# Four PSUM banks for the projection units, three staging slots and a gate row summed in sixteen pieces

## Time and profile before

| what | value |
|---|---|
| median of 3 runs | 865.06 us |
| profiled execution, its own time | 870.05 us |
| its span, first to last instruction | 868.2 us |
| PE busy | 772.1 us, 89% |
| DVE, ACT, POOL busy | 517.9, 455.3, 393.0 us |
| mean granted TensorE clock | 0.956 |

### The profile page before, as it was taken

How to read it: one execution, slowest core, us unless ns; L and a number is a source line. 1 busy time by engine, 2 the same in 40 slices (tenths; PEclk the granted TensorE clock), 3 DMA queues, 4 the chain that set the end, 5 groups by cost and what they waited for, 6 DMA issues and landing times.

```text
span 868.2 us, 9916 instructions
## 1 busy us (share of the span) xinstructions
PE 772.1 (89%) x3468; PEld 614.3 (71%) x3468; DVE 517.9 (60%) x716; ACT 455.3 (52%) x749; POOL 393.0 (45%) x405
## 2 busy tenths in 40 slices
PE   6596898999779889889998899699989699999996
PEld 2275687888668768777776787477668478888885
DVE  4389752646873878595776333665534477666633
ACT  4265642887755875766774675334525253434311
POOL 0268553475555763765546446424300235252521
PEclk9897899999988999999998999899999999999999
DMA  9994013245524254343443123344328765858541
GB/s 367 352 298 136 25 38 122 61 105 134 157 70 119 72 165 152 107 129 102 147 143 103 55 92 112 110 134 134 107 80 322 243 222 183 286 170 264 172 134 74
DMA packets 89073, 130.09 MB, mean 150 GB/s; under 512 B 22752, under 2 KB 54112, under 8 KB 87488
## 3 DMA queue, kind: packets, MB, share of 16 engines
q1 hardware_dynamic: 84656, 115.44, 40.7%
q0 software_dynamic: 4368, 14.03, 5.8%
HBM read 91.17 MB, written 38.27 MB: 149 GB/s over the span
## 4 chain that ended last, share of the span: by engine, by line
PE 44%; ACT 15%; DVE 14%; issue 10%; POOL 7%; DMA 6%; SPq 4%; ACTq 0%; POOLq 0%; DVEq 0%
PE bank L1443 14%; PE bank L1444 14%; PE bank L1445 14%; SPq L403 2%; ACT L942 2%; ACT Qb L943 2%; DVE Qb L1267 2%; ACT bank L944 2%; ACT Ib L930 2%; DMA wraw<-in_w_in 2%; DVE gacc L1120 1%; DVE xg L1153 1%; DVE xc L1120 1%; DVE xTl L1171 1%; DVE Ib L1257 1%
## 5 line engine op out<-in xcount | busy, mean ns | idle before, releaser
L1443 PE MATMUL bank<-xTh,wh 128*128 128x512 f32 (+1 forms) x592 | 239.3, 404 | 40.8 <-ACT ustage L917 11.6
L1445 PE MATMUL bank<-xTh,wl 128*128 128x512 f32 (+1 forms) x592 | 236.1, 399 | 0.0
L1444 PE MATMUL bank<-xTl,wh 128*128 128x512 f32 x576 | 231.9, 403 | 0.0
L1443 PEld LDWEIGHTS bank<-xTh,wh 128*128 128x128 f32 x592 | 116.1, 196 | 68.9 <-issue 42.2
L1445 PEld LDWEIGHTS bank<-xTh,wl 128*128 128x128 f32 x592 | 115.5, 195 | 24.7
L1444 PEld LDWEIGHTS bank<-xTl,wh 128*128 128x128 f32 x576 | 112.9, 196 | 23.8 <-issue 0.2
L1443 PE MATMUL bank<-xTh 128*128 128x512 f32 (+1 forms) x272 | 106.8, 392 | 14.1 <-DVE xTl L1391 7.2
L1445 PE MATMUL bank<-xTh,xTl 128*128 128x512 f32 x256 | 99.9, 390 | 0.0
L1444 PE MATMUL bank<-xTl,xTh 128*128 128x512 f32 x256 | 99.7, 390 | 0.0
L917 ACT ACTIVATE ustage<-bank 128x512 f32<-128x512 f32 x56 | 33.5, 600 | 120.1 <-PE bank L1445 116.0
L569 POOL TENSOR_SCALAR xTh<-yb 128x512 fp32r<-128x512 f32 x32 | 19.8, 619 | 122.1 <-DVE yb L1389 122.1
(11 more groups left out here) (189 smaller groups left out, 1520.1 us busy)
## 6 DMA issues: line engine op xcount, KB each, us to landing
scratch_u<-ustage SPq DMA_DIRECT2D x72, 256.0 KB, 2.9
wraw<-in_w_in SPq DMA_DIRECT2D x18, 512.0 KB, 4.2
wm<-in_w_mod SPq DMA_DIRECT2D x8, 1024.0 KB, 11.7
xg<-in_x SPq DMA_DIRECT2D x16, 512.0 KB, 8.8
yb<-scratch_y SPq DMA_DIRECT2D x32, 256.0 KB, 3.1
gb<-scratch_u SPq DMA_DIRECT2D x32, 256.0 KB, 4.4
xres<-in_x SPq DMA_DIRECT2D x16, 512.0 KB, 4.8
out<-tout SPq DMA_DIRECT2D x16, 512.0 KB, 2.9
```

What stands on the lines that cost most here:

```text
L1443: mm(out, wh_, xh_, start=first, stop=False)
L1444: mm(out, wh_, xl_, start=False, stop=False)
L1445: return mm(out, wl_, xh_, start=False, stop=last)
```

## The change

- The units of the middle (units 8 to 67, `WIDE`) go in turn through four banks, 0, 1, 6, 7, so that a unit waits for the evacuation of the one four before it. The others keep two banks.
- `gr` is one pair, banks 2 and 3. `one_minus_a2` writes its result over `Qb` in SBUF, the root is taken there, and the product with `Ib` reads it there. `gates(q)` waits for `one_minus_a2(q-1)` instead of `scans(q-2)`.
- `ustage` has three slots, with a semaphore each.
- The gate row's weights come in sixteen pieces of 128 x 4 x 128, each summed in its own step, 3 to 18. The rule for where a piece is loaded is as before, and so is the wait for the sum of the piece before it; a `dve.wait_ge` is added behind each sum.
- In the tail the LayerNorm root is taken in place in `lvar` and read from there (`lsd` is gone); the next variance waits for the products that read it; the first mean waits for `one_minus_a2(19)`; the first two pooling products wait for the evacuation of the wide units.

```diff
+U_SLOTS = 3
...
-GATE_STEP = [3 + 2 * m for m in range(8)]
+WIDE = range(N_CU + 2 * NCH, N_CU + GATES_AFTER[-1] + 1)
+PU_BANK = [(0, 1, 6, 7)[U % 4] if U in WIDE else U % 2 for U in range(N_CU + len(UNITS))]
+
+
+def evacuations_before(U):
+
+    earlier = [V for V in range(U) if PU_BANK[V] == PU_BANK[U]]
+    return earlier[-1] + 1 if earlier else 0
+
+
+GATE_STEP = [3 + m for m in range(16)]
 GATE_PIECE_AT = [GATES_AFTER[q - 1] + 1 for q in GATE_STEP]
...
-        wgp = a3.take("wgp", [P, KD, P])
+        wgp = a3.take("wgp", [P, KD // 2, P])
...
-        pu = bank[0:2]
-        gr = [bank[2:4], bank[6:8]]
+        pu = [bank[b] for b in PU_BANK]
+        gr = bank[2:4]
...
                 for o in range(2, NT_IN):
                     if n == LAST_OF[o - 2]:
                         load_w(o + 2)
-                for m in range(KD):
+                for m in range(2 * KD):
                     if n == GATE_PIECE_AT[m]:
                         if m:
                             sp.wait_ge(s_ga, m)
-                        sp.dma_start(wgp[:], w_mod[8 + m // 2, :, :, m % 2 * P:m % 2 * P + P]).then_inc(s_wg, 16)
+                        b, h = divmod(m, 2)
+                        part = w_mod[8 + b // 2, :, h * KD // 2:(h + 1) * KD // 2, b % 2 * P:b % 2 * P + P]
+                        sp.dma_start(wgp[:], part).then_inc(s_wg, 16)
...
-                if U >= 2:
-                    act.wait_ge(s_us[U % 2], 16 * (U // 2))
+                if U >= U_SLOTS:
+                    act.wait_ge(s_us[U % U_SLOTS], 16 * (U // U_SLOTS))
...
-                    r = gr[q % 2][d][:, 0:n]
-                    a.activation(r, r, ACT.Sqrt).then_inc(s_rt, 1)
+                    root = Qb[:, d, 0:n]
+                    a.activation(root, root, ACT.Sqrt).then_inc(s_rt, 1)
...
-                    r = gr[q % 2][d][:, 0:n]
-                    stt(r, Qb[:, d, 0:n], 1.0, r, ALU.add, ALU.mult).then_inc(s_m2, 1)
+                    stt(Qb[:, d, 0:n], Qb[:, d, 0:n], 1.0, gr[d][:, 0:n], ALU.add, ALU.mult).then_inc(s_m2, 1)
...
-                    link(v.tensor_tensor(out=I, in0=I, in1=gr[q % 2][d][:, 0:n], op=ALU.mult))
+                    link(v.tensor_tensor(out=I, in0=I, in1=Qb[:, d, 0:n], op=ALU.mult))
...
-                acc = gacc[:, m * P:(m + 1) * P]
-                link(v.tensor_scalar(acc, wgp[:, 0, :], cs[:, 0:1], None, ALU.mult))
-                for k in range(1, KD - 1):
-                    link(stt(acc, wgp[:, k, :], cs[:, 2 * k:2 * k + 1], acc, ALU.mult, ALU.add))
-                k = KD - 1
-                stt(acc, wgp[:, k, :], cs[:, 2 * k:2 * k + 1], acc, ALU.mult, ALU.add).then_inc(s_ga, 1)
+                b, h = divmod(m, 2)
+                acc = gacc[:, b * P:(b + 1) * P]
+                for k in range(KD // 2):
+                    scale = cs[:, 2 * (h * KD // 2 + k):2 * (h * KD // 2 + k) + 1]
+                    if h == 0 and k == 0:
+                        ins = v.tensor_scalar(acc, wgp[:, k, :], scale, None, ALU.mult)
+                    else:
+                        ins = stt(acc, wgp[:, k, :], scale, acc, ALU.mult, ALU.add)
+                    if k < KD // 2 - 1:
+                        link(ins)
+                ins.then_inc(s_ga, 1)
+                dve.wait_ge(s_ga, m + 1)
...
-                if U >= 2:
-                    pe.wait_ge(s_ev, U - 1)
+                if evacuations_before(U):
+                    pe.wait_ge(s_ev, evacuations_before(U))
...
                 if q:
                     pe.wait_ge(s_sig, 4 * q)
-                if q >= 2:
-                    pe.wait_ge(s_st, 2 * (q - 1))
+                    pe.wait_ge(s_m2, 2 * q)
```

More of the change, by code:

```diff
@@ L128, in mixer_kernel @@
         wl = fixed.take("wl", [P, 2, KD, P], f32r)
-        ustage = fixed.take("ustage", [P, 2, CH])
+        ustage = fixed.take("ustage", [P, U_SLOTS, CH])
         prm = fixed.take("prm", [P, N_PAR])
@@ L269, in mixer_kernel @@
         s_pu, s_ev = sem("unit_done"), sem("unit_evacuated")
-        s_us = [sem(f"u_stored{b}") for b in range(2)]
+        s_us = [sem(f"u_stored{b}") for b in range(U_SLOTS)]
         s_gz, s_gw, s_gwh, s_gwl = sem("gatew_zeroed"), sem("gatew_in"), sem("gatew_hi"), sem("gatew_lo")
@@ L444, in store_u @@
                 if U < N_CU:
[L445 removed]
+                    dst, src = uc_dram[U], ustage[:, U % U_SLOTS, 0:CTX]
                 elif o == "conv":
[L447 removed]
+                    dst, src = cv_dram[c], ustage[:, U % U_SLOTS, 0:NPH]
                 elif ORDER[o] in CONV_TILES:
                     dst = phases(u_dram[ORDER[o]], NPH)[:, :, c * CH // PHASES:(c + 1) * CH // PHASES]
[L450 removed]
+                    src = phases(ustage[:, U % U_SLOTS, :], CH // PHASES)
                 else:
[L452 to L453 removed]
+                    dst, src = u_dram[ORDER[o], :, c * CH:(c + 1) * CH], ustage[:, U % U_SLOTS, :]
+                sp.dma_start(dst, src).then_inc(s_us[U % U_SLOTS], 16)
             def load_conv_w(j):
@@ L627, in load_v @@
                     U = unit_of(V_LRU + t, NCH - 1)
-                    for back in (0, 1):
-                        pool.wait_ge(s_us[(U - back) % 2], 16 * ((U - back) // 2 + 1))
+                    for back in range(U_SLOTS):
+                        pool.wait_ge(s_us[(U - back) % U_SLOTS], 16 * ((U - back) // U_SLOTS + 1))
                     off = a - (c * CH - 2)
@@ L715, in load_ln @@
                 else:
-                    for U in range(N_CU + CONV_AT[-1] - 1, N_CU + CONV_AT[-1] + 1):
-                        pool.wait_ge(s_us[U % 2], 16 * (U // 2 + 1))
+                    for U in range(N_CU + CONV_AT[-1] + 1 - U_SLOTS, N_CU + CONV_AT[-1] + 1):
+                        pool.wait_ge(s_us[U % U_SLOTS], 16 * (U // U_SLOTS + 1))
                 part = slice(n * CH // PHASES, (n + 1) * CH // PHASES)
@@ L1045, in ln_root @@
                     act.wait_ge(s_lzn, 2 * m)
-                a.activation(lsd[:], lvar[:], ACT.Sqrt, bias=lnepsc).then_inc(s_lsd, 1)
+                a.activation(lvar[:], lvar[:], ACT.Sqrt, bias=lnepsc).then_inc(s_lsd, 1)
             def ln_swish(m):
@@ L1368, in ln_norm @@
                 dve.wait_ge(s_lsd, n + 1)
-                link(v.reciprocal(lsd[:], lsd[:]))
+                link(v.reciprocal(lvar[:], lvar[:]))
                 for i in range(2):
                     z = lr[:, n % 2, i, :]
-                    v.tensor_tensor(out=z, in0=z, in1=lsd[:], op=ALU.mult).then_inc(s_lzn, 1)
+                    v.tensor_tensor(out=z, in0=z, in1=lvar[:], op=ALU.mult).then_inc(s_lzn, 1)
             def ln_lo(n):
@@ L1507, in gates @@
                     pe.wait_ge(s_sig, 4 * q)
-                if q >= 2:
-                    pe.wait_ge(s_st, 2 * (q - 1))
+                    pe.wait_ge(s_m2, 2 * q)
                 for m in range(4):
                     d = 0 if s == 0 else m // 2
-                    b = gi_[m // 2] if m % 2 else gr[q % 2][m // 2]
+                    b = gi_[m // 2] if m % 2 else gr[m // 2]
                     ins = mm3(b[:, 0:n], gwh[:, m, :], gwl[:, m, :], sph[:, d, 0:n], spl[:, d, 0:n], True, True)
@@ L1577, in _ @@
                         pe.wait_ge(s_pye, n - 1)
+                    else:
+                        pe.wait_ge(s_ev, WIDE.stop)
                     mm3(pmb[n % 2][:], pwh[:, i, :], pwl[:, i, :], pdh[:], pdl[:], True, True).then_inc(s_pmm, 1)
```

31 lines of the change are left out of this document (15 added, 16 removed).

## The result

The changed kernel took **925.09 us** in the median of four runs (923.79 to 925.97), the kernel before 867.33 on the same chip (864.12 to 872.48): a ratio of 1.066 [1.060, 1.072]. It is slower, as forecast, but by 58 us and not by 28: 925 lies above the range (874 to 914).

What follows compares the result with a forecast made beforehand. It took PE's pauses on two banks, branch A's loop over ACT and DVE, and SP's weight transfers to bound the kernel. 41.4 - 2 - 13 + 2 = +28 us on the median 865.06 gave 893 us, range 874 to 914.

Steps and rivals of the forecast that it cites:

- SP's new wait: Steps 3 to 17: SP stops behind its first store until the step's scans and gate sum end; +41.4 us, less 2.
- Steps 10 to 12 and 17: Middle: weights wanted only some 9 us later, so SP's wait is covered; 0, or 1 to 2 us a step if not.
- Terms of the loop: Added us, sigmoids to sigmoids: step 7 +6.4, 14 +6.8, 8 +8.5, 13 +5.2, 15 +9, 6 +6, 16 -3.5, 3 +3.
- Four banks win: Rival: half of the 54 us bound from PE's pauses and low clock is gained, giving 838 us; chance 0.09.
- Even: Rival: SP's wait hurts only steps 7 and 14, +14, tiles' delay covered, -13 comes back; around 866 us; chance 0.10.
- DVE and POOL in each other's way: Rival: in eight loops sum operations take 2 us rather than 0.35 and products stretch; 919 us; chance 0.12.
- Four banks: Middle: PE's pauses go where nothing else binds; 9 us in steps 10 to 12, 4 in 17 and 18, hence -13.
- the tail: End of kernel: a variance waits for the reciprocal, 3.35 us, and two products, but this is hidden; 0.
- the new wait of `gates(q)`: PE waits for `one_minus_a2(q-1)`; 0 to 1 us a step in short steps 1 to 5, taken as 0.
- the third slot: Evacuations need the store three units back, issued before SP's stop, so the slot hides what it should; no cost.
- Root and product in SBUF: Branch A: roots +0.1 us each, 1 to 3 in all; products stretched 0 to 1.1 each, taken as 1; together +2.

Runs made afterwards that it cites:

- The pieces alone: The kernel before with only the sixteen half pieces of the gate row (two banks, two slots, both pairs kept): 928.23 us, 1.067.
- the late piece: The changed kernel whole, each piece asked for one step later, so the sum it waits for lies a step back: 858.45 us, 0.987.
- the experiment with their stops alone: The late piece with pieces asked for as early as in the changed kernel in steps 10, 11 and 12 only: 870.10 us, 1.002.

## Why the prediction was right in direction and wrong in size

**SP's new wait: right.** The pieces alone bring the whole loss, asking a step later takes it all back. The lists of waits name the releaser that was forecast, over the 15 stops forecast. The 161.4 us are above the 60 to 110 given: much of it is time in which SP would have stood anyway. Up to 22 us behind the first sigmoid of step 19 its waits for evacuations fell from 331 us to 220, so its waits in all rose by some 50.

**Step that failed first: "Steps 10 to 12 and 17: the weights are wanted only after the next decays, some 9 us later, so SP's wait is covered."** It held for 17 (with 18: -7.6), not for 10 to 12: forecast -9 with the banks, measured +8.0. The profiled executions differ by 55 us, 27 more than the sum of 28, and 17 of these 27 lie here. SP's stops cost 11.8 of them (63.9 against 52.1 with the late piece), where the prediction had 0, and 1 to 2 a step if the cover were gone; its "some 9 us later" came from no row. Steps 11 and 12 hold 6.4 of the 11.8, and the experiment with their stops alone shows such a loss: 7.5 in steps 10 to 12, and 4.4 more in step 13. The other 5.4 lie in step 10. And the gain was at most 3.8 (55.9 to 52.1) and not 9, which is the rest of the 17. In step 12 of the changed kernel, ACT:

```profile
424.09 1.06 ACT L879 ACTIVATE wh<-wraw 128x1024 fp32r<-128x1024 f32 x1 [7.30 <-DMA wraw<-in_w_in]
...
427.57 1.15 ACT L964 ACTIVATE Qb<-Qb 128x512 f32<-128x512 f32 x2
```

SP:

```profile
414.54 0.38 SPq L496 DMA_DIRECT2D wgp<-in_w_mod  x1
...
417.54 0.37 SPq L425 DMA_DIRECT2D wraw<-in_w_in  x1
```

The cover was real and too short. The scans of step 11 ended 7 us into step 12, the sum at 414.5, the tile was issued at 417.5 and landed after 6.5 us, when ACT had stood for 7.3. And it was wanted ahead of the roots, so the scans of step 12 were late too and carried it into step 13. I had compared the cover with SP's wait alone and not with the wait, the six issues ahead of the tile's (3.0 us) and the transfer together. With the pieces alone, on two banks, these steps took 55.5 us against 55.9 before, so that no cost of the stops shows there; whether the cover held or the longer step 9 ahead of them had taken the delay was not tried. Step 10 lost 4.2 us against the kernel before by a second way, through the weight behind the stop of step 9, a stop that the prediction put at 0 and that was not tried apart: POOL waited for the rounded convolution weight, and behind it on POOL stood the next input of the convolution on DVE:

```profile
364.45 2.11 POOL L700 TENSOR_TENSOR cvwl<-cvwraw,cvwh 128x640 fp32r<-128x640 f32 x1 [10.79 <-ACT cvwh L977]
...
370.49 0.54 POOL L643 DMA_DIRECT2D vbuf<-scratch_u  x1
```

**Terms of the loop: mechanism right, sizes low.** Steps 7, 13 and 14 were forecast at 18.4 us more and took 31.0. Of the 12.6 us between, some 4.4 are the sum: 4 x 0.35 = 1.4 was forecast, and it took 3.5 us in step 7, 2.7 in step 13 and 2.4 in step 14. I took the median of a lopsided distribution, where a group's cost needs the mean. All 64 operations of the changed kernel:

```profile
L1132 DVE SCALAR_TENSOR_TENSOR gacc<-wgp,sml,gacc 128x128 f32<-128x128 f32 x56 | 36.9, 659 | 1.9
...
L1310 DVE TENSOR_SCALAR gacc<-wgp,sml 128x128 f32<-128x128 f32 x8 | 8.1, 1011 | 0.2
```

45.0 us for 16 sums, 2.8 us each. In step 14 it was mostly the transfer of the convolution weight, 5.8 us against 3.1 read from a single row; the issue on SP and its reader on ACT:

```profile
484.82 0.57 SPq L469 DMA_DIRECT2D cvwraw<-in_conv_dw  x1
```

```profile
490.62 0.74 ACT L977 ACTIVATE cvwh<-cvwraw 128x640 fp32r<-128x640 f32 x1 [12.41 <-DMA cvwraw<-in_conv_dw]
```

In step 13 it was mostly the scans, which ended 21.6 us behind the first sigmoid and not 15.4: 1.9 us are a wait for the scans of step 12 and 3.7 a wait for the convolution weight behind the stop of step 12. Its tile took 5.0 us, no more than forecast. Steps 8 and 15 came out below their terms (26.9 against 28.5; 24.6 against 27), step 6 two above, steps 3 and 4 at the upper end of 0 to 6, since the four operations of that sum took 6.1 us, about what two of the eight had taken before; I had counted on a sum half as long.

**The rivals.** *Four banks win* fell as a forecast for this kernel, but the gain is there once SP is free: 11 us, not 27. *Even* fell: the tiles' delay was not covered. *DVE and POOL in each other's way* described part of the missing size, the sums of 2.8 us, but not the cause; it gave 919 by way of the loops, and the larger share was lost in steps that it left out, so its nearness to 925 is luck.

**Four banks: right for the waits, wrong for half of the place.** PE's waits for `ustage` went as forecast. Steps 17 and 18 gained 7.6 where I took 4; 3.8 of that is what four banks bring with the late piece. But steps 10 to 12, with 9 of the 13 us, take 52.0 us with two banks and 52.1 with four: nothing. What four banks gain lies in steps 6, 9, 17 and 18. In all the 33.6 us of the earlier trace rows are worth 8 us and not 13: most of what went came back as waits for POOL.

**Costed at nothing:** the tail, the new wait of `gates(q)`, the third slot. The tail took 351.4 us against 350.1. The other two were not tried apart, but the kernel with both, two banks and the late piece stands at 0.996, so neither shows a cost. **Root and product in SBUF:** +2 forecast, 0 measured; the mean product grew from 0.68 to 0.87 us, within the bound, and off the path. Of the 40 products of the changed kernel the longest took 1.8 us. The root took 0.62 us in SBUF against 0.58 in PSUM (medians of 40), below the +0.1 taken.

## What to carry to other kernels

A semaphore wait on a queue that issues transfers costs what stands behind it, not what it guards: list each transfer behind the wait, when its reader wants it, and add up wait, issues and landing before calling it covered. When a job is cut into more and smaller pieces, check in which step the event now lies that each piece waits for; here it slid from one step back into the same step and closed a loop. Work a cover out again for each schedule. Cost a group of operations with a long tail by their mean.

## What the runs showed of the hardware

- **Two operands in SBUF.** With the product's second operand in PSUM none of 40 took over 0.690 us; with root and product moved to SBUF and nothing else changed, the 32 of 512 columns went from 0.681 on average to 0.869, and the eight of 256 columns from 0.416 to 0.822. In that run the seven longest products (1.45 to 2.03 us) each overlap an operation of POOL, six of them its `cvwl`. The two long sum operations of step 7, from 306.96 to 309.53, fall together with two `spl` operations of POOL, which read SBUF:

```profile
306.76 2.62 POOL L666 TENSOR_TENSOR spl<-xc,sph 128x512 fp32r<-128x512 f32 x2
```

  1.28 us for a 128-column operation is then the length of a POOL operation of 1.3 us. POOL had no operand in PSUM in any row of the traces before and after. This fits what the Trainium skill says (SBUF — State Buffer, section on SBUF's two separate sides): a VectorE operation with two SBUF inputs and a GpSimd operation that reads SBUF exclude each other for a whole instruction.
- **Landing.** Where ACT stood waiting for it, a 128 x 1024 weight tile of 0.5 MB took 4.2 to 6.6 us from issue to use in the changed kernel and 3.7 to 5.2 before, a 128 x 640 one 3.6 to 5.8 and 3.1 to 4.9. The 3.1 that the prediction took from a single row stood against 5.8 in step 14.
